# Splitting the state-space output product into three reduced-precision products, with the norm's factor applied at the eviction

## The reference

```python
y = rmsnorm(y.reshape(bsz, seq_len, SSD_INNER) * jax.nn.silu(z), ssd_norm_w)
mix = jnp.concatenate([o_gla, y], axis=-1)
h = h + mix @ w_out
h = h + peer(rmsnorm(h, norm2_w), peer_wq, ...)
```

## Time and profile before

| | us |
|---|---|
| median of 3 runs | 1998.92 (1998.65 to 2000.63) |
| the profiled execution | 2001.23 |
| its span, first to last instruction | 1999.1 |
| TensorE busy in it | 1966.5 |
| VectorE, ScalarE, GpSimd busy | 1222.8, 635.5, 1108.5 |

### The profile page before, as it was taken

How to read it: one execution, slowest core, us unless ns; L and a number is a source line. 1 busy time by engine, 2 the same in 40 slices (tenths; PEclk the granted TensorE clock), 3 DMA queues, 4 the chain that set the end, 5 groups by cost and what they waited for, 6 DMA issues and landing times.

```text
span 1999.1 us, 28689 instructions
## 1 busy us (share of the span) xinstructions
PE 1966.5 (98%) x10893; PEld 1763.8 (88%) x10893; DVE 1222.8 (61%) x2259; ACT 635.5 (32%) x935; POOL 1108.5 (55%) x694
## 2 busy tenths in 40 slices
PE   8999999989999999999999999999999999999997
PEld 4688778868999999999999999999999999999996
DVE  4544456656897887778243341115677777777775
ACT  3333113223333232323223333223333333333332
POOL 0213210122368787888888888866566666666310
PEclk9999998899999999999999999999999999999999
DMA  4494113033345455565555556788999999999971
GB/s 153 155 343 154 43 33 80 3 110 112 106 126 119 132 119 132 113 142 122 134 129 126 126 127 155 174 194 279 319 332 321 330 323 327 329 321 327 335 252 49
DMA packets 237284, 365.15 MB, mean 183 GB/s; under 512 B 87777, under 2 KB 178418, under 8 KB 236530
## 3 DMA queue, kind: packets, MB, share of 16 engines
q1 hardware_dynamic: 163570, 294.37, 44.2%
q0 software_dynamic: 72448, 67.41, 16.2%
q10 hardware_dynamic: 1152, 1.84, 0.3%
HBM read 290.15 MB, written 73.38 MB: 182 GB/s over the span
## 4 chain that ended last, share of the span: by engine, by line
PE 96%; DVE 3%; ACT 1%; issue 0%; DMA 0%; DVEq 0%; SPq 0%; ACTq 0%
PE bank L974 31%; PE bank L1058 31%; PE bank L603 9%; PE bank L983 9%; PE bank L918 2%; PE bank L891 2%; PE bank L846 1%; PE bank L621 1%; PE bank L729 1%; PE bank L701 1%; PE bank L745 1%; PE bank L965 1%; PE bank L834 1%; DVE xn L1401 1%; PE bank L1018 1%; PE bank L614 1%
## 5 line engine op out<-in xcount | busy, mean ns | idle before, releaser
L1941 POOL DMA_INDIRECT gates_scratch<-gate_val,gate_at x384 | 643.9, 1677 | 138.1 <-issue 115.5
L1058 PE MATMUL bank<-W,vsp 128*128 128x448 f32 x3072 | 623.0, 366 | 0.0
L1058 PEld LDWEIGHTS bank<-W,vsp 128*128 128x128 f32 x3072 | 577.4, 188 | 45.0
L974 PE MATMUL bank<-xh,usp 128*128 128x448 f32 x2048 | 594.2, 366 | 0.0
L974 PEld LDWEIGHTS bank<-xh,usp 128*128 128x128 f32 x2048 | 385.2, 188 | 29.9 <-issue 0.2
L974 PE MATMUL bank<-xl,usp 128*128 128x448 f32 x1024 | 374.5, 366 | 0.0
L1707 DVE TENSOR_TENSOR usp<-ring,usp 128x1024 fp32r<-128x1024 f32 x120 | 144.5, 1221 | 329.0 <-ACT usp L1255 328.7
L1817 DVE TENSOR_TENSOR vsp<-ring,vsp 128x1024 fp32r<-128x1024 f32 x128 | 157.0, 1227 | 179.9 <-ACT vsp L1342 179.9
L1960 POOL DMA_INDIRECT picked<-in_v,row_index x128 | 149.4, 1167 | 185.4 <-DVE acc L1836 162.4
L1967 POOL DMA_INDIRECT hid_b<-own_hidden_scratch,hid_index x128 | 189.5, 1481 | 59.0 <-issue 38.7
L974 PEld LDWEIGHTS bank<-xl,usp 128*128 128x128 f32 x1024 | 192.7, 188 | 14.0
(11 more groups left out here) (293 smaller groups left out, 2044.4 us busy)
## 6 DMA issues: line engine op xcount, KB each, us to landing
ring<-in_u SPq DMA_DIRECT2D x128, 512.0 KB, 3.7
ring<-in_v SPq DMA_DIRECT2D x128, 512.0 KB, 5.6
hidden_scratch<-gl SPq DMA_DIRECT2D x128, 224.0 KB, 1.9
xn<-hidden_scratch SPq DMA_DIRECT2D x128, 224.0 KB, 5.8
G<-gates_scratch SPq DMA_DIRECT2D x120, 224.0 KB, 4.8
gates_scratch<-zero SPq DMA_DIRECT2D x32, 768.0 KB, 8.6
ring<-in_wproj SPq DMA_DIRECT2D x36, 512.0 KB, 3.9
own_hidden_scratch<-glo SPq DMA_DIRECT2D x64, 128.0 KB, 1.7
```

What stands on the lines that cost most here:

```text
L974: mm = pe.matmul(bank[b][:, 0:TA], w, src[:, k, 0:TA], start=(k == 0 and w is hi and src is xh), stop=(k == KT - 1 and w is lo))
L1058: mm = pe.matmul(bank[(k + 4) % 8][:, 0:TA], w, W[:, n % 4, z, :], start=(n == 0 and w is hi and z == 0), stop=(n == NE - 1 and w is lo))
L1941: pool.indirect_dma_start(gates_flat, bass.IndirectOffsetOnAxis(ap=gate_at[0:r, i, x:x + 1], axis=0), gate_val[0:r, i, hh, x - hh * TOPK:x ...
```

## The change

The SSD tiles are no longer multiplied by the norm's factor before the product. ScalarE writes `mix * ssd_w`, rounded to float32r, into `out_x[0]` (`gated_square`), VectorE the remainder into `out_x[1]`; ScalarE rounds each tile's weights into `out_w[:, k % 2, 0]` (`split_out`), GpSimd subtracts to get the low part (`low_out`). `project_ssd` sums high by high, low rows by high weights and high rows by low weights. VectorE multiplies the sum by the reciprocal root when it reads the bank (into `part`) and adds it to `h` in a second instruction. TensorE's GLA products of tiles 6 and 7 are set between the partition sums, and GpSimd's low parts of the query weights wait for the whole loop. SP's program is as before.

```diff
@@ tensor
-                if k % 2 == 0:
-                    pe.wait_ge(ring_loaded[k // 2], 16 * (N_FEAT // 4 + 2))
+                pe.wait_ge(qlo_ready, k + 1)
                 wait_proj_evacuated(pe, n)
                 for x in range(2):
                     for c in range(4):
-                        a = k % 2 * (D // 2) + c * P
-                        mm = pe.matmul(bank[2 * (n % 2) + x][:, 0:HALF], ring[:, k // 2, a:a + P],
-                                       mix[:, 4 + c, x * HALF:(x + 1) * HALF], start=(c == 0), stop=(c == 3))
+                        for w, y in ((0, 0), (0, 1), (1, 0)):
+                            mm = pe.matmul(bank[2 * (n % 2) + x][:, 0:HALF], out_w[:, k % 2, w, c * P:(c + 1) * P],
+                                           out_x[y][:, c, x * HALF:(x + 1) * HALF], start=(c == 0 and w == 0 and y == 0),
+                                           stop=(c == 3 and w == 1))
...
             pe.wait_ge(y_copied, TILES)
-            for k in range(4):
-                norm_sum(1, k)
+            norm_sum(1, 0)
+            norm_sum(1, 1)
             project_gla(TILES + 1)
+            norm_sum(1, 2)
+            norm_sum(1, 3)
             project_gla(TILES + 2)
-            pe.wait_ge(half_copied, KT)
             pe.wait_ge(normed, norm_base[1] + 4)
             for k in range(KT):
                 project_ssd(k)
                 if k == 0:
+                    pe.wait_ge(half_copied, KT)
                     to_state(4, 0)
                 to_state(4, k + 1)
@@ scalar
+            def gated_square(k):
+                act.wait_ge(yz_ready, k + 1)
+                if k >= 2:
+                    act.wait_ge(sq_used, norm_base[1] + k - 1)
+                act.activation(sq[:, k % 2, :], mix[:, 4 + k, :], ACT.Square).then_inc(sq_ready, 1)
+                act.activation(out_x[0][:, k, :], mix[:, 4 + k, :], ACT.Copy, scale=pp("ssd_w")[:, k:k + 1]).then_inc(xh_ready, 1)
+
+            def split_out(k):
+                act.wait_ge(ring_loaded[k // 2], 16 * (N_FEAT // 4 + 2))
+                if k >= 2:
+                    act.wait_ge(proj_done, N_FEAT + k - 1)
+                act.activation(out_w[:, k % 2, 0, :], ring[:, k // 2, k % 2 * (D // 2):(k % 2 + 1) * (D // 2)], ACT.Copy
+                               ).then_inc(qhi_ready, 1)
+
+            act.wait_ge(y_done, TILES)
+            split_out(0)
+            split_out(1)
+            gated_square(0)
+            gated_square(1)
             copy_gla_out(TILES)
-            norm(1, lambda k: act.wait_ge(yz_ready, k + 1))
+            gated_square(2)
+            gated_square(3)
             copy_gla_out(TILES + 1)
+            norm_roots(1)
             copy_gla_out(TILES + 2)
...
+                if k + 2 < KT:
+                    split_out(k + 2)
                 act.wait_ge(proj_dve, k + 1)
@@ vector
-            dve.wait_ge(yz_ready, 4)
-            norm(1)
+            for j in range(4):
+                dve.wait_ge(xh_ready, j + 1)
+                dve.scalar_tensor_tensor(out_x[1][:, j, :], mix[:, 4 + j, :], pp("ssd_w")[:, j:j + 1],
+                                         out_x[0][:, j, :].bitcast(F32), ALU.mult, ALU.subtract).then_inc(normed, 1)
+            root(1)
...
-                dve.wait_ge(x_added, k + 1)
                 dve.wait_ge(proj_done, n + 1)
                 for x in range(2):
-                    ins = dve.tensor_tensor(h[:, k, x * HALF:(x + 1) * HALF], h[:, k, x * HALF:(x + 1) * HALF],
-                                            bank[2 * (n % 2) + x][:, 0:HALF], ALU.add)
-                ins.then_inc(proj_dve, 1)
+                    ins = dve.tensor_tensor(part[:, x * HALF:(x + 1) * HALF], bank[2 * (n % 2) + x][:, 0:HALF],
+                                            sq[:, 0, x * HALF:(x + 1) * HALF], ALU.mult)
+                link(ins)
+                dve.wait_ge(x_added, k + 1)
+                dve.tensor_tensor(h[:, k, :], h[:, k, :], part[:, :], ALU.add).then_inc(proj_dve, 1)
                 new_state(4, k)
@@ gpsimd
+            def low_out(k):
+                pool.wait_ge(qhi_ready, k + 1)
+                pool.tensor_tensor(out_w[:, k % 2, 1, :], ring[:, k // 2, k % 2 * (D // 2):(k % 2 + 1) * (D // 2)],
+                                   out_w[:, k % 2, 0, :].bitcast(F32), ALU.subtract).then_inc(qlo_ready, 1)
+
+            low_out(0)
+            low_out(1)
             pool.wait_ge(x_reloaded, 16 * KT)
             for k in range(KT):
                 pool.wait_ge(half_copied, k + 1)
                 pool.tensor_tensor(h[:, k, :], h[:, k, :], gla_out[k], ALU.add).then_inc(x_added, 1)
+            for k in range(2, KT):
+                low_out(k)
+            pool.wait_ge(proj_done, N_FEAT + KT)
             for n in range(N_FEAT + KT + 1, N_PROJ):
-                pool.wait_ge(qhi_ready, n - N_FEAT - KT)
+                pool.wait_ge(qhi_ready, n - N_FEAT)
```

More of the change, by code:

```diff
@@ L253, in build @@
         mix_stack.close()
+        outs = ExitStack()
+        sb(outs, "sg_place", [P, 8 * T + 4 * T])
+        out_x = [sb(outs, "out_high", [P, 4, T], F32R)]
+        sb(outs, "small_place", [P, 6136])
+        out_x.append(sb(outs, "out_low", [P, 4, T], F32R))
+        sb(outs, "btok_place", [P, 5568])
+        out_w = sb(outs, "out_w", [P, 2, 2, D // 2], F32R)
+        part = sb(outs, "part", [P, T])
+        outs.close()
         row_index = sb(base, "row_index", [P, PH * TOPK], U32)
@@ L416, in build @@
         norm_base = [0, KT, KT + 4, 2 * KT + 4]
-        norm_par = ["norm1", "ssd_w", "norm2", "final"]
+        norm_par = {0: "norm1", 3: "final"}
         Lf = L[:, :, :, :].rearrange("p a h t -> p (a h t)")
@@ L946, in _ @@
             for n in range(N_FEAT + KT + 1, N_PROJ):
-                pe.wait_ge(qlo_ready, n - N_FEAT - KT)
+                pe.wait_ge(qlo_ready, n - N_FEAT)
                 wait_proj_evacuated(pe, n)
@@ L1084, in norm, with norm_roots @@
             def norm(m, ready):
-                src, n = norm_src[m]
-                off = 4 if m == 1 else 0
-                for k in range(n):
+                src = norm_src[m][0]
+                for k in range(KT):
                     ready(k)
[L1090 to L1097, removed]
+                    if k >= 3:
+                        act.wait_ge(sq_used, norm_base[m] + max(1, k - 3))
+                    act.activation(square(m, k), src[:, k, :], ACT.Square).then_inc(sq_ready, 1)
+                norm_roots(m)
+            def norm_roots(m):
+                n = norm_src[m][1]
                 act.wait_ge(sq_used, norm_base[m] + n)
@@ L1393, in norm @@
             def norm(m):
-                src, n = norm_src[m]
-                off = 4 if m == 1 else 0
-                dst = mix if m == 1 else xn
+                src = norm_src[m][0]
                 if m > 0:
@@ L1399, in norm @@
                 w = pp(norm_par[m])
-                for k in range(n):
-                    dve.scalar_tensor_tensor(dst[:, off + k, :], src[:, off + k, :], w[:, k:k + 1], sq[:, 0, :],
+                for k in range(KT):
+                    dve.scalar_tensor_tensor(xn[:, k, :], src[:, k, :], w[:, k:k + 1], sq[:, 0, :],
                                              ALU.mult, ALU.mult).then_inc(normed, 1)
@@ L1662, in _ @@
             segment_rows(1)
-            dve.wait_ge(yz_ready, 4)
-            norm(1)
+            for j in range(4):
[3 more added lines that the diff above has]
+            root(1)
+            dve.wait_ge(y_done, TILES)
             for k in range(KT):
@@ L1681, in low_x @@
             def low_x(k):
-                dve.wait_ge(xh_ready, k + 1)
+                dve.wait_ge(xh_ready, 4 + k + 1)
                 dve.tensor_tensor(xl[:, k, :], xn[:, k, META:T], xh[:, k, :].bitcast(F32), ALU.subtract).then_inc(xl_ready, 1)
```

## The result

| | before | after |
|---|---|---|
| median of 16 runs each, us | 2001.78 (1998.65 to 2002.67) | 2004.13 (2002.54 to 2005.81) |
| ratio, 95% interval | | 1.0016 [1.0009, 1.0023] |
| span of the profiled execution | 1999.1 | 2003.8 |

The ratio is +3.2 us of 2001.78, from +1.8 to +4.6; the two medians differ by 2.35. The forecast was +2.7 and 2001.6, its range reached to 2005.7. The 16 runs of the kernel before have a median 2.9 above that of the three that the forecast stood on, and so the difference came out better than the level.

A forecast was written before the change was run, and what follows sets the result against it. TensorE's path was taken as the bound, ending 96% of the span; start 5.3, loop -6.6 and tail +3.95 gave +2.7 us on a median of 1998.92, so 2001.6, range 1996.3 to 2005.7.

The forecast's parts named there:

- Start: Last SSD token tile to first SSD product: ScalarE's splits wait for the weight load, first product at 424.4, 5.3 late.
- The bound of 426.4: First SSD product's latest start, if the return of TensorE's clock takes another 4 us; the forecast was 424.4.
- Rival 3: Start: ScalarE's wait is short, the load landing by 402; -6.2 us in all, 1992.7; chance 0.04.
- Loop: First to last SSD product: faster float32r products, 34.2 us instead of 40.8, -6.6; bounds 33.2 and 38.3.
- 2 x 4.15 and 4 x 4.4: Loop's six turns: first two at TensorE's 4.15 us, four late ones at 4.4 with VectorE partly waiting for POOL.
- rival 2: Loop: VectorE becomes the bound, each turn paying the whole 1.1; +6.8 us in all, 2005.7; chance 0.15.
- the full 1.1: Loop: most that VectorE's added addition waits per turn for POOL's subtraction, making 5.0 us a turn.
- Tail: Last SSD product to next norm's reciprocals: POOL's low parts exclude VectorE's work, 8.2 us instead of 4.24, +3.95.
- Rival 1: Loop and tail: exclusion weak, turns at 4.15, tail +0.7; -1.6 us in all, 1997.3; chance 0.2.
- The sum: Whole stage: start 5.3, loop -6.6 and tail +3.95 make +2.7 us, 2001.6.
- the three stretches: Last SSD token tile to first product, the loop, and the tail to the reciprocals; their changes sum to the forecast.

The follow-up runs named there:

- e1: Changed kernel with the first two ring loads of SSD weights issued ahead of the reloads of `h`: 1991.94 us, 0.9959 of the kernel before.
- e3: Changed kernel with GpSimd's subtraction cut to 32 of 512 columns from tile 2 on (output differs): 2003.25 us, 1.0006 of the kernel before.
- e2: Changed kernel with GpSimd's query-weight low parts waiting for the last state update instead of the last product: 2001.67 us, 1.0002 of the kernel before.
- e10: The changed kernel itself, unaltered, run again on another experiment's chip: 2005.32 us, 1.0018 of the kernel before.
- e5: Changed kernel with two SSD weight loads ahead of the `h` reloads and query-weight low parts behind the last state update: 1990.98 us, 0.9949 of the kernel before.
- e4: Changed kernel with an unsplit fp32 product, factor still at the eviction, query-weight low parts released as before the change: 1995.88 us, 0.9970 of the kernel before.
- e8: Kernel before with the first two ring loads of SSD weights issued ahead of the residual reload: 2001.94 us, 0.9999 of the kernel before.

## Why the prediction was right

**Start: the mechanism held, its size was 1.3 us short.** Three terms were off, and a fourth partly made up for them. The load landed 7.6 us after its issue, not 6.7, so the first sum began at 411.15 instead of 410.4 (0.75). The clock came back 5.5 us after TensorE resumed (411.15 to 416.7) instead of 3.9, so GLA tile 6 ran partly at 1.2 GHz and took 4.7 (415.23 to 419.94) instead of 4.0. The two sums at low clock took 0.2 more, and what followed 0.3 less. The bound of 426.4, "if its return takes another 4 us", held it. Low rows took 1.79 each, low weights were done by 412.5, and neither was waited for; the reciprocals cost nothing, as said. e1 shows that the wait was the load's: without it 12.4 us are back. Rival 3, a short wait, is out: the split began at 409.27. One reading of the rows was incomplete: TensorE's timeline of the kernel before has a fourth gap, 0.91 us before GLA tile 7 at 412.16, which the prediction doesn't count; no term of its sum uses it.

**Loop: right in kind, 1.2 short.** The chain gives a product 3.29 us, the forecast from the earlier trace rows. VectorE was held from the first of the six turns on, before any square is added, so six turns of 4.44 stood where 2 x 4.15 and 4 x 4.4 had been put (0.75); 0.2 lies in the first two products and states, and 0.2 in the mark of the loop's end (40.6 for 40.8). The chain lies on VectorE from 434.81 on: rival 2 was right that VectorE sets the turns, and wrong in the price. It wasn't the full 1.1 in each, because GpSimd starts only after TensorE's product and ScalarE's split: turns that VectorE makes late shift it against GpSimd, and additions of 1.5 and 1.0 alternate. At 440.29 GpSimd's pass (439.30 to 440.64) has 0.35 us left when the addition begins, and it takes 0.99; at 453.35 the pass has 0.89 left, and it takes 1.52. e3 measures the exclusion by taking it away, 0.32 a turn.

**Tail: right, +3.5 for +3.95.** The addition begins 0.9 after GpSimd's first pass and takes 2.08, its own 0.78 behind the rest of that pass; the state's update takes 2.84 behind the second. The Trainium skill, "SBUF — State Buffer", section "SBUF: two separate sides", says that VectorE with two SBUF inputs and GpSimd take their shared ports as a lock for a whole instruction. The trace agrees: 2.08 against 0.78, 2.84 against 0.69, and 0.83 for the instruction whose one input is in a bank. Rival 1, weak exclusion, is out by e2 and e3: where GpSimd is moved or cut the same instructions fall to 0.69 and 0.78.

**The sum.** The three errors, 1.3 + 1.2 - 0.4, make the 2.1 by which the three stretches (4.7) lie above the forecast (2.7). Over all runs the difference is smaller: 3.2 by the ratio, 2.35 by the medians. The spans overstate it, because the profiled execution of the changed kernel (2005.55) lies 1.4 above its median and that of the kernel before 0.55 below. The repetition e10, profiled at its median, has the same loop (35.15) and tail (7.95) and a start that is 0.7 shorter: counted from the GLA tile's start, where the first profile gives +4.9, it is 4.1 above the kernel before, and 3.75 in the medians. So the terms came out 1.5 to 2 us above the forecast, and that the ratio's 3.2 lies as near to it as it does is in part luck.

## What to carry to other kernels

On an engine that runs in order, a new wait is priced by what stands behind it: moving its load ahead on SP was worth 12 us in the changed kernel, and nothing that the runs show in the kernel before, where nothing waited for that load. The faster products paid 3.7 us in the loop (e5 against e4), although GpSimd's passes met VectorE's two-input additions there at 0.32 a turn. In the tail the same meeting cost 2.7 us: GpSimd's passes over SBUF should not be released by the event that VectorE's critical instruction waits for. Time the parts of a change apart: here 6 us of gain and a larger loss came in as one change of 0.16%.

## What was not expected of the hardware

TensorE's clock came back after very different times: 3.9 us after resuming in the kernel before, 2.9 in e8 (420.07 to 423.0, by a mean of 0.75 over 422 to 424), 4.3 in the repetition of the changed kernel, 5.5 in its first profile. It also fell at different times ahead of the change, where all these kernels do the same. The stretches of e1:

```profile
384.00:386.00 2.00, 2.00 (x20) 2.00 (x20) 0.00 (x0) 0.00 (x0) 0.00 (x0) 1.00 0.00 0
386.00:388.00 2.00, 2.00 (x15) 2.00 (x15) 0.00 (x0) 0.00 (x0) 0.00 (x0) 0.72 0.00 0
```

Those of the kernel after:

```profile
384.00:386.00 2.00, 2.00 (x20) 2.00 (x19) 0.00 (x0) 0.00 (x0) 0.00 (x0) 0.99 0.00 0
386.00:388.00 2.00, 2.00 (x11) 2.00 (x11) 0.00 (x0) 0.00 (x0) 0.00 (x0) 0.50 0.00 0
```

It fell while TensorE was busy for the whole of these 2 us, with the products of 16 to 160 columns of `sample_heads`. Where it fell later, the GLA tile behind began at 392.39 instead of 395.17; 1.0 of these 2.8 us stood already when those products began (380.71 against 381.71), and 1.8 came during them. Differences of 1 to 3 us between single profiles can come from this; the stretches of the experiments were therefore measured from a start inside each trace. Why the clock falls when it does was not tried.
